# One stage for mixers and attention: mLSTM steps between attention units

## What is computed

```python
hf, Cf, nf, mf = mlstm_chunkwise(qh, kh, vh, ...)           # forward, 4 heads x 64, chunks of 128
hb, Cb, nb_, mb = mlstm_chunkwise(rev(qh), rev(kh), ...)    # backward
ml_out = jax.nn.sigmoid(mo) * (hf + rev(hb)).reshape(B, T, ML_WIDTH)
cm_out = chunk_spatial_gating(cu, cv, p['cm_norm_g'], p['cm_ws'], p['cm_b'])
q = (rmsnorm(cq, p['mla_q_norm_g']) @ p['mla_w_uq'])        # 8 heads, 64 + 32 rotary
k_nope, vals = mla_kv(ckv_n, p['mla_w_ukv'])                # plus a cached tile of 128 keys
att = mla_attention(q_nope, q_rope, k_nope, k_rope, vals)   # softmax attention
mix = jnp.concatenate([ml_out, cm_out, att], axis=-1) @ p['w_out']
```

## Time and profile before

| | us |
|---|---|
| median of three runs | 4059.56 (4057.76 to 4061.55) |
| the profiled execution | 4058.4, span of its instructions 4056.6 |
| layer 1: gate rows and spatial gating | 212.7 to 254.5 |
| layer 1: ten mLSTM steps | 254.5 to 344.2 |
| layer 1: query, key and value products | 344.2 to 401.5 |
| layer 1: 40 attention units | 401.5 to 501.4 |
| PE busy over the span | 3578.2 (88%) |
| DVE busy over the span | 3443.1 (85%) |

### The profile page before, as it was taken

How to read it: one execution, slowest core, us unless ns; L and a number is a source line. 1 busy time by engine, 2 the same in 40 slices (tenths; PEclk the granted TensorE clock), 3 DMA queues, 4 the chain that set the end, 5 groups by cost and what they waited for, 6 DMA issues and landing times. The chain is left out here.

```text
span 4056.6 us, 60199 instructions
## 1 busy us (share of the span) xinstructions
PE 3578.2 (88%) x20120; PEld 3211.3 (79%) x20120; DVE 3443.1 (85%) x7161; ACT 1400.3 (35%) x2436; POOL 1995.4 (49%) x1520
## 2 busy tenths in 40 slices
PE   3978989188999999999968889882899999999996
PEld 3955789177999999999867758882789999999995
DVE  7954749898999999999969456598989999999997
ACT  3321332084333333333333123312833333333332
POOL 0000023196777777777600001223867777777773
PEclk9957989599999999999978599996999999999998
DMA  6721011148999999999757010102499999999995
GB/s 230 233 69 42 1 44 43 43 186 327 405 405 405 402 393 404 399 398 400 304 180 231 2 42 22 44 22 94 197 382 405 406 406 404 391 405 401 399 399 213
DMA packets 303611, 1032.16 MB, mean 254 GB/s; under 512 B 30793, under 2 KB 82825, under 8 KB 296401
## 3 DMA queue, kind: packets, MB, share of 16 engines
q0 software_dynamic: 147456, 536.94, 33.5%
q1 hardware_dynamic: 155986, 493.13, 32.2%
HBM read 976.40 MB, written 53.56 MB: 254 GB/s over the span
## 5 line engine op out<-in xcount | busy, mean ns | idle before, releaser
L1529 POOL DMA_INDIRECT picked_rows<-in_u_rows,chosen x512 | 790.2, 1543 | 414.5 <-DVE dots_now L1805 187.1
L1529 POOL DMA_INDIRECT picked_rows<-in_v_rows,chosen x512 | 811.3, 1585 | 258.9 <-DVE y L1813 141.4
L1702 PE MATMUL ps<-hd_hi,u_hi 128*128 128x384 f32 x2048 | 698.4, 341 | 24.5 <-DVE a_lo L1795 15.2
L1702 PE MATMUL ps<-hd_hi,u_lo 128*128 128x384 f32 x2048 | 696.1, 340 | 0.0
L1702 PE MATMUL ps<-hd_lo,u_hi 128*128 128x384 f32 x2048 | 695.4, 340 | 0.0
L1813 DVE SCALAR_TENSOR_TENSOR y<-picked_rows,dots_now,y 128x1024 f32<-128x1024 f32 x512 | 643.9, 1278 | 0.0
L1805 DVE CUSTOM_DVE_ANT_0 picked_rows<-picked_rows,h2rows 128x1024 f32<-128x1024 f32 x512 | 614.2, 1218 | 0.0
L1105 POOL TENSOR_TENSOR wout_lo<-wout,wout_hi 128x2048 fp32r<-128x2048 f32 x8 | 36.8, 4595 | 924.4 <-ACT wout_hi L1084 924.4
L1713 PE MATMUL ps<-v_hi,a_hi 128*128 128x512 f32 x1536 | 479.0, 393 | 0.0
L1713 PE MATMUL ps<-v_hi,a_lo 128*128 128x512 f32 x1536 | 475.1, 390 | 0.0
L1713 PE MATMUL ps<-v_lo,a_hi 128*128 128x512 f32 x1536 | 473.2, 389 | 0.0
(11 more groups left out here) (306 smaller groups left out, 6897.7 us busy)
## 6 DMA issues: line engine op xcount, KB each, us to landing
u_raw<-in_u SPq DMA_DIRECT2D x256, 512.0 KB
v_raw<-in_v SPq DMA_DIRECT2D x256, 512.0 KB
mod_ring<-in_ada SPq DMA_DIRECT2D x96, 512.0 KB, 4.4
gates_dram<-gmat SPq DMA_DIRECT2D x12, 4096.0 KB, 11.6
gt<-gates_dram SPq DMA_DIRECT2D x64, 768.0 KB
w_raw<-in_w_in SPq DMA_DIRECT2D x18, 1024.0 KB, 6.1
wq<-in_wq SPq DMA_DIRECT2D x8, 2048.0 KB, 8.1
wout<-in_w_out SPq DMA_DIRECT2D x8, 1024.0 KB, 7.4
```

What stands on the lines that cost most here:

```text
L1529: pool.indirect_dma_start(picked_rows[:, n % RING, :], None, a[table], bass.IndirectOffsetOnAxis(ap=chosen[:, m % GT, m // GT:m // GT + 1] ...
L1702: ins = pe.matmul(ps[:, b % 2, 0:TD], (u_hi, u_lo)[wl][:, b % 2, k, :], (hd_hi, hd_lo)[hl][:, k, :], start=(k == 0 and n == 0), stop=(k == ...
```

## The change

`mixers` and `attention` become one stage, `mix`, without a barrier between them.

- The query products and ACT's copies of them move ahead of the spatial gating, to stand beside DVE's gate rows. ACT now copies all 128 rows to SBUF, and DVE turns two heads at a time from SBUF, right behind the gate rows and ahead of the spatial gating's results.
- Steps 0 to 2 of the mLSTM stand between key and value products; steps 3 to 9 stand between the first 14 attention units, one step for two units (`SHARED = 14`). The other 26 units run as before.
- A step is cut in three on PE: `lead` (mask and `r_u`), `middle` (scores) and `back` (numerator, new state, old state). An even unit carries a `middle`, an odd one a `back` and the next `lead`.
- PSUM is divided: weights and scores of a step share bank 5, its results banks 6 and 7, attention transposes banks 2 and 3, attention results bank 4. In the first 14 units all scores use banks 0 and 1, so scores(n+1) come after turn(n) and need the exponentials of unit n done.
- The mask of the four heads is one product of 512 columns instead of four of 128. Within the scores and within the old-state part PE waits on its own semaphore `upper_rows` after the second head.
- SP loads `w_out`'s first parts after the key and value products, and `gate1` and `wq` after the last unit. POOL's clearing of the mixer semaphores moves into `retrieve`. SBUF homes are set by byte offsets (`place`), and `proj` is split in `proj_a` and `proj_b`.

The core of the diff (queries, key products with steps, units with steps on PE, and the self-wait):

```diff
-                    pe.wait_ge(q_dve, h - 1)
+                pe.wait_ge(q_act, AH)
+                lead(0)
+                for h in range(AH):
+                    key_products(h)
+                    if h == 1:
+                        middle(0)
+                    if h == 3:
+                        back(0)
+                        lead(1)
+                    if h == 5:
+                        middle(1)
+                back(1)
+                lead(2)
...
+                def middle(n):
+                    s, d, t = place_of(n)
+                    span = slice(t * P, (t + 1) * P)
+                    pe.wait_ge(w_exp, n + 1)
+                    for m in range(H):
+                        hp, hh = m // 2, m % 2
+                        part = slice(hp * HD, (hp + 1) * HD)
+                        ins = pe.matmul(ps[:, 5, m * P:(m + 1) * P], mkT[part, hh, span], mqT[part, hh, span],
+                                        start=True, stop=True)
+                        if m == 1:
+                            ins.then_inc(upper_rows, 1)
+                            pe.wait_ge(upper_rows, 2 * n + 1)
+                    ins.then_inc(st_psum, 1)
...
                 def scores(n):
-                    b = 2 * (n % 2)
-                    if n >= 2:
-                        pe.wait_ge(p_ready, n - 1)
+                    b = score_bank(n)
+                    if n >= 1:
+                        pe.wait_ge(p_ready, n if n <= SHARED else n - 1)
...
                 scores(0)
-                for n in range(len(units)):
-                    if n + 1 < len(units):
+                for n in range(SHARED):
+                    turn(n)
+                    scores(n + 1)
+                    m = AHEAD + n // 2
+                    if n % 2 == 0:
+                        middle(m)
+                    else:
+                        back(m)
+                        if m + 1 < STEPS:
+                            lead(m + 1)
+                    attend(n)
```

And on DVE, the rotation behind the gate rows and the shared loop:

```diff
+                for h in range(0, AH, 2):
+                    dve.wait_ge(q_act, h + 2)
+                    link(dve.tensor_tensor(rot[HD:QK, :, :], qT[QK:P, h:h + 2, P:T],
...
+                for n in range(SHARED):
+                    turned(n)
+                    maxima(n + 1)
+                    m = AHEAD + n // 2
+                    if n % 2 == 0:
+                        weighted(m)
+                    else:
+                        taken(m)
+                    finish(n)
+                link(dve.tensor_tensor(mixed[:, :, 0:256], mixed[:, :, 0:256], bwd[:, :, :], ALU.add))
```

More of the change, by code:

```diff
@@ new lines, in _, with scores @@
+                back(1)
+                lead(2)
+                pe.wait_ge(k_act, AH)
+                for t in range(KT):
+                    value_products(t)
+                    if t == 2:
+                        middle(2)
+                back(2)
+                lead(3)
+                pe.wait_ge(v_dve, KT)
+                pe.wait_ge(kr_ready, 1)
+                pe.wait_ge(q_turned, AH // 2)
+                def scores(n):
+                    h, t = units[n]
+                    lo, hi, _ = keys(t)
+                    b = score_bank(n)
+                    if n >= 1:
+                        pe.wait_ge(p_ready, n if n <= SHARED else n - 1)
+                    if n == SHARED + 1:
+                        pe.wait_ge(nd_taken, STEPS)
+                    q = qT[0:QK, h, t * P:(t + 1) * P]
+                    mid = min(hi, lo + 512)
+                    ins = pe.matmul(ps[:, b, 0:mid - lo], q, kT[0:QK, h, lo:mid], start=True, stop=True)
+                    if hi > mid:
+                        ins = pe.matmul(ps[:, b + 1, 0:hi - mid], q, kT[0:QK, h, mid:hi], start=True, stop=True)
+                    ins.then_inc(s_psum, 1)
@@ new lines, in turn, with attend @@
+                def turn(n):
+                    h, t = units[n]
+                    pe.wait_ge(p_ready, n + 1)
+                    if n >= 1:
+                        pe.wait_ge(pt_taken, n)
+                    for i in range(len(keys(t)[2])):
+                        ins = pe.transpose(ps[:, 2 + i // 4, (i % 4) * P:(i % 4 + 1) * P], prob[:, n % 2, i * P:(i + 1) * P], ident[:, :])
+                    ins.then_inc(pt_psum, 1)
+                def attend(n):
+                    h, t = units[n]
+                    pe.wait_ge(pt_taken, n + 1)
+                    if n >= 1:
+                        pe.wait_ge(o_taken, n if n <= SHARED else n - 1)
+                    tiles = keys(t)[2]
+                    for i, kt in enumerate(tiles):
+                        ins = pe.matmul(ps[:, out_bank(n), 0:HD], probT[:, n % 2, i * P:(i + 1) * P], val[:, kt, h * HD:(h + 1) * HD],
+                                        start=(i == 0), stop=(i == len(tiles) - 1))
+                    ins.then_inc(o_psum, 1)
@@ new lines, in _ @@
+                scores(0)
+                for n in range(SHARED):
[9 more added lines that the diff above has]
+                    attend(n)
+                for n in range(SHARED, UNITS):
+                    if n + 1 < UNITS:
+                        scores(n + 1)
+                    turn(n)
+                    if n > SHARED:
+                        attend(n - 1)
@@ L758, in _, with weights @@
                 act.wait_ge(cols_taken, 1)
[L759 to L761 removed]
+                act.wait_ge(early_out, 48)
+                act.wait_ge(sgu_taken, NT)
+                def weights(n):
+                    s, d, t = place_of(n)
                     act.wait_ge(w_psum, n + 1)
@@ L1125, in maxima @@
+                weighted(2)
+                for t in range(3, KT):
+                    values(t)
+                taken(2)
                 def maxima(n):
```

716 lines of the change are left out of this document (319 added, 397 removed).

## The result

| | before | changed kernel |
|---|---|---|
| median | 4059.57 (4055.52 to 4061.88, 20 runs) | 4039.26 (4013.28 to 4061.03, 20 runs) |
| ratio of the times, 95% interval | | 0.9948 (0.9932 to 0.9965) |
| profiled execution | 4058.4 | 4026.6 (span 4024.8) |
| layer 1: `dec` in SBUF | 254.5 | 269.5 |
| layer 1: first exponentials of the units end | 401.9 | 330.6 |

The changed kernel is faster, by 0.5%. It is also less even: its times spread over 48 us, those of before over 6.

The account below looks back on a forecast made before the run. PE was taken to bound both the mLSTM steps, at half clock, and the attention units. Later queries, full-clock steps and the shared loop summed to 28.6 us a layer, 57 in all: 4059.6 to 4002, range 3980 to 4066.

Parts of the forecast that it names:

- Part 1: Queries moved beside the gate rows: columns (`dec`) in SBUF at 270.9, 16.4 us later, in place of 22.3 for queries.
- Part 2: Price of one mLSTM step in the new form at full clock: 5.75 us, against 8.4 at half clock.
- Part 3: From columns to the first attention unit, with keys, values and three steps: 57.2 us, so first unit at 328.1.
- Part 4: Shared loop of steps and 14 units 77 us, two DVE products 3, remaining 26 units 64.7; last unit at 472.8.
- its 28.6: Microseconds by which the last attention unit would come earlier in each layer, 472.8 against 501.4.
- The moved DMAs: Loads of `gate1`, `wq` and first parts of `w_out` at new places: hidden, at no cost; `gate1` uncovered 2.7 us.
- the projection: Output projection after the last unit: no change in its time was counted.
- The clock: PE clock in the shared loop: starts warm, only standing still lowers it, so 1.00 taken throughout.
- Rival B: Small products let the clock fall in the shared loop: wholly cold 61 us more a layer, 4124; chance 0.18.
- Rival C: Queues in the shared loop couple badly and PE waits: a pair of units 14.2 instead of 11.85, 4046; chance 0.13.
- Rival D: PE's self-waits in the steps nearly free, a step costs 4.4, handovers hide: 3980; chance 0.11.

Follow-up runs that it names:

- e2_full_queries: e1_fullrows with query products, copies and rotation put back behind the columns, as in the kernel before: 4013.2 us, ratio 0.9886.
- e2_before_full: Kernel before the change, with only its selector products run over 128 rows (92 of them zero) instead of 36: 3981.38 us, ratio 0.9803.
- e4_look_a: The changed kernel, unedited, profiled again for one more trace: 4035.8 us.
- e1_fullrows: Changed kernel with the selector products of a lead over 128 rows (92 of them zero) instead of 36: 3996.33 us, ratio 0.9848.
- e2_full_apart: e1_fullrows with steps 3 to 9 run by themselves ahead of the first attention unit: 4134.18 us, ratio 1.0181.
- e4_look_b: The changed kernel, unedited, profiled once more for a fourth trace: 4045.3 us.

## Why the prediction was wrong, step by step

**Part 1 held.** `dec` at 269.5 for 270.9; the 1.4 are the gate rows, which ended 1.5 earlier (239.5 for 241.0), and from there to `dec` it took 30.0 for 29.9. The move is worth about what it was said to be (`e2_full_queries`).

**Part 2 held as a sum, with one twist.** Scores 1.40 for 1.35, back 2.63 for 2.6, lead 1.41 for 1.8, at full clock: 5.44 for 5.75. But that price was compared with the 8.4 of a step at half clock only. The old step at full clock, 4.2, stood in the text as a bound and was never asked after as an alternative. `e2_before_full` measured 4.11: the new form made a step 1.3 dearer. The self-waits alone account for it, with 0.75 in the scores and 0.70 in the old state.

**Part 3 was off by 3.9**: 61.1 from `dec` to the first exponentials (330.6 less 269.5) instead of 57.2. With the clock held it was 53.3 (322.0 less 268.7). The clock was down from 290 to 294 and from 307 to 315, among keys and steps, with PE busy.

**Part 4 was off by 5.4 in the profiled run** (82.4 instead of 77, with 21.5 at half clock) and by 21 in `e4_look_a`. In `e1_fullrows` the loop took 74.5. The DVE products cost 3.0 and a further cold stretch, the 26 units 66.7 for 64.7. Together with Parts 1 and 3 this is the whole shortfall of the profiled run: 3.9 + 5.4 + 2.0, less the 1.4 of Part 1, are 9.9 of the 10.0 us by which layer 1 missed its 28.6.

**The moved DMAs held, the projection not quite**: nothing waits for `gate1`, but the projection starts at half clock and takes 2.2 us more.

**The clock is the step that failed.** The text said that small products do not raise it but that only standing still lowered it, "in what I read", and took 1.00 throughout. The reading was of a kernel in which dense and small products never met. There the 89.7 us at 0.50 were the warning: a busy PE that stays at half clock for that long shows that this work does not hold the clock, and half of the shared loop is the same work. Rival B was the right mechanism, too cheap in chance, and its condition too narrow: it was priced as a loop cold or warm, not as one that changes from run to run. Its price was right: 61 us for a loop of 138 cold ones are 0.44 for each, and 0.45 were measured. And the time came out on the faster side not because the clock held, but because the loop was cold for a part of its length only. The rule of the Trainium skill, "TensorE: Matmul & The Clock Gate", "Part 1: The HAM clock gate (the "warmup" mystery)", that sustained activity releases the throttle, fails here in one more way than the forecast said: PE was busy 57.21 of 58 us in `e4_look_a` at 0.50. The same section of the Trainium skill says that one kernel measures 6, 11 or 14 slow matmuls at its start in different runs. Here too the cold part differs between runs, but in the middle of the kernel and by more: 21.5 us of the loop in one run and 58 in another.

With the clock held in most of the stage, the forecast would have come out about right: `e1_fullrows` took 3996 where 4002 were said, with some 6 us of its gain from shorter leads.

**Rival C, the coupling, is small.** The waits of PE in the shared loop of the changed kernel, in total, times and longest:

```profile
PE ps L835 <- ACT prob L942: 3.0, 3, 2.4
```

That is all that the table of waits has for PE from 330.5 to 413, and 2.4 of it is the wait at the loop's start. **Rival D**, free self-waits, is refuted: they add 0.75 to the scores (1.47 for 0.72) and 0.70 to the old state (1.37 for 0.67), before the clock.

**What stays open.** Which microsecond the clock falls in, in a given run, I cannot tell from the traces. Nor is it shown whether full rows in the scores and the old state too would mend the 7 us behind the standstill. Nor whether it is PE's standing or the self-waits that kept `e2_full_apart` at half clock. A shared loop without self-waits wasn't tried; by my reading of the kernel it needs two banks more than are left.

## What to carry to other kernels

Where a stage runs at half clock with PE busy, first ask why, and try to lift the clock in place (here: zeros up to 128 rows, at no cost in instructions, 78 us; up to 96 rows brought 16 of them without the clock) before moving work to where the clock is high. Price the old order at full clock too, since that is the true rival of a new order. Small products set between dense ones can drag the clock down as well as be lifted by it; a spread of times that grows from 6 to 48 us is the sign.

## What the hardware did that I had not expected

- The ten steps of the old order, with PE busy in all cases, ran at 0.50 with selector products on 36, 64 and 96 rows, and at 1.00 with 128, of which 92 hold zeros. So rows of zeros counted for the clock; rows of data in their place weren't tried.
- Products on rows 0 to 63 and on 64 to 127 that run side by side belong to that: with a wait between them, the steps fell back to 0.54 though the leads were on 128 rows; forty such waits cost 96.5 us in all.
- A pair of a 128-row mask and a selector product took 0.3 us longer at half clock with the selector on 36 or 64 rows than on 96 (0.95 between masks for 0.64).
- A busy PE lost the clock in the middle of its work: at 290 and at 307 in the first profile, and at 2360 in `e4_look_b` behind a wait of only 0.32 us. How long it stays down changes from run to run: 58 us of the loop at 0.50 in one run, 21.5 in another, the same instructions.
